# A two-layer block on one core: the triangular solve in blocks of 32 rows, one weight split on GpSimd, and the pair of FFN inputs interleaved in SBUF

## The reference

```python
def _rwkv7_step(S, inp):
    r, w, k, v, a, b = inp
    sa = jnp.einsum('bhvk,bhk->bhv', S, a)
    S = S * w[:, :, None, :] + sa[..., None] * b[:, :, None, :] + v[..., None] * k[:, :, None, :]
    y = jnp.einsum('bhvk,bhk->bhv', S, r)
    return S, y
...
    mean = jnp.mean(y, axis=-1, keepdims=True)
    var = jnp.mean(jnp.square(y - mean), axis=-1, keepdims=True)
    yn = ((y - mean) * lax.rsqrt(var + LNX_EPS)).reshape(B, T, D) * lnx_w + lnx_b
    bonus = (jnp.sum(rh * kh * r_k, axis=-1, keepdims=True) * vh).reshape(B, T, D)
    out = ((yn + bonus) * g).astype(x.dtype)
    return out @ w_o

def conv_ffn(x, w_in, conv_w, conv_b, w_out):
    T = x.shape[1]
    gate, up = jnp.split(x @ w_in, 2, axis=-1)
    gp = jnp.pad(gate, ((0, 0), (CONV_W - 1, 0), (0, 0)))
    gc = conv_b
    for j in range(CONV_W):
        gc = gc + gp[:, j:j + T, :] * conv_w[j]
    h = jax.nn.gelu(gc) * up
    return h @ w_out
```

## Time and profile before

| | |
|---|---|
| median of 3 runs | 1096.93 us (1094.85 to 1100.52) |
| the profiled execution, its own time | 1099.76 us |
| its span | 1097.9 us |
| granted clock, mean | 0.997 |
| PE busy | 1071.0 us (98%) |
| DVE busy | 801.8 us (73%) |
| ACT busy | 605.1 us (55%) |
| POOL busy | 209.3 us (19%) |

### The profile page before, as it was taken

The page is one execution under the profiler, slowest core; times in us unless marked ns, Lnnn a source line. Parts: engine busy times, 40 slices in busy tenths (PEclk is TensorE's granted clock), DMA queues, the critical chain, the costliest instruction groups (busy, mean ns, idle before and its releaser), DMA issues.

```text
span 1097.9 us, 19100 instructions
## 1 busy us (share of the span) xinstructions
PE 1071.0 (98%) x7335; PEld 924.8 (84%) x7335; DVE 801.8 (73%) x1134; ACT 605.1 (55%) x928; POOL 209.3 (19%) x230
## 2 busy tenths in 40 slices
PE   7999989999999999999999999999999999999997
PEld 6997788888888889789888888998777789888886
DVE  7997887778885758777788746688867776655543
ACT  6765354556664566856566544635665445545532
POOL 0134552112221011001222200470100001122200
PEclk9999999999999999999999999999999999999999
DMA  8553181646666566345667575456452654666552
GB/s 250 170 170 115 46 262 43 172 116 192 185 189 228 196 148 161 118 130 146 188 188 194 174 286 158 155 192 213 148 140 83 194 166 131 184 189 191 192 191 77
DMA packets 219748, 183.13 MB, mean 167 GB/s; under 512 B 43265, under 2 KB 197614, under 8 KB 219678
## 3 DMA queue, kind: packets, MB, share of 16 engines
q1 hardware_dynamic: 215710, 171.43, 52.1%
q0 software_dynamic: 3392, 8.66, 2.5%
q10 hardware_dynamic: 576, 2.07, 0.5%
HBM read 179.44 MB, written 2.69 MB: 166 GB/s over the span
## 4 chain that ended last, share of the span: by engine, by line
PE 82%; DVE 12%; issue 2%; ACT 1%; POOL 1%; DMA 1%; SPq 0%; DVEq 0%; POOLq 0%; ACTq 0%
PE bank L288 21%; PE bank L282 13%; PE bank L284 13%; PE bank L283 13%; PE bank L289 10%; PE bank L295 3%; DVE ring L413 3%; PE bank L1238 2%; DVE arena L1655 1%; DVE arena L1750 1%; DVE stat L1748 1%; PE bank L371 1%; PE bank L2123 1%; PE bank L1353 1%; DVE arena L1680 0%
## 5 line engine op out<-in xcount | busy, mean ns | idle before, releaser
L413 DVE TENSOR_TENSOR ring<-ring,arena 128x2048 fp32r<-128x2048 f32 (+1 forms) x138 | 312.3, 2266 | 113.0 <-ACT arena L407 111.4
L282 PE MATMUL bank<-arena 128*128 128x512 f32 (+3 forms) x980 | 343.8, 351 | 2.0 <-DVE ring L413 1.6
L288 PE MATMUL bank<-arena 128*128 128x512 f32 x960 | 339.8, 399 | 0.0
L407 ACT ACTIVATE arena<-ring 128x2048 fp32r<-128x2048 f32 (+1 forms) x145 | 272.0, 1879 | 93.0 <-DMA ring<-in_ffn_w_out 43.2
L289 PE MATMUL bank<-arena,ring 128*128 128x256 f32 x960 | 269.6, 281 | 0.0
L284 PE MATMUL bank<-arena 128*128 128x512 f32 (+3 forms) x720 | 264.9, 368 | 0.0
L288 PEld LDWEIGHTS bank<-arena 128*128 128x128 f32 x960 | 180.4, 188 | 44.7
L283 PE MATMUL bank<-ring,arena 128*128 128x512 f32 (+2 forms) x560 | 216.2, 386 | 0.0
L282 PEld LDWEIGHTS bank<-arena 128*128 128x128 f32 x980 | 185.5, 189 | 27.1 <-issue 3.7
L289 PEld LDWEIGHTS bank<-arena,ring 128*128 128x128 f32 x960 | 181.5, 189 | 0.0
L284 PEld LDWEIGHTS bank<-arena 128*128 128x128 f32 x720 | 135.6, 188 | 22.3
(11 more groups left out here) (335 smaller groups left out, 1282.7 us busy)
## 6 DMA issues: line engine op xcount, KB each, us to landing
ring<-in_ffn_w_in SPq DMA_DIRECT2D x80, 512.0 KB, 5.1
ring<-in_ffn_w_out SPq DMA_DIRECT2D x44, 512.0 KB, 4.4
ring<-in_w_gate_up SPq DMA_DIRECT2D x40, 512.0 KB, 5.1
ring<-in_w_in SPq DMA_DIRECT2D x18, 1024.0 KB, 5.0
ring<-in_a_w_rkv SPq DMA_DIRECT2D x12, 1024.0 KB, 5.5
ring<-in_w_down SPq DMA_DIRECT2D x22, 512.0 KB, 3.7
ring<-in_a_w_o SPq DMA_DIRECT2D x4, 1024.0 KB, 8.4
arena<-in_ffn_w_in SPq DMA_DIRECT2D x8, 512.0 KB, 4.7
```

The lines of the kernel that those rows point to most:

```text
L282: nc.tensor.matmul(dst, stationary[0], moving[0], start=start, stop=False)
L288: nc.tensor.matmul(dst[:, :], stationary[0], both_parts, start=start, stop=False)
L407: nc.scalar.activation(buf(hi_of(n), 0, w, arena12), ring[:, r, 0:w], ACT.Copy).then_inc(hi_ready, 1)
L413: on.tensor_tensor(ring12[:, r, 0:w], ring[:, r, 0:w], buf(hi_of(n), 0, w, arena12).bitcast(F32), ALU.subtract).then_inc(split_ready, 1)
```

## The change

- **Solve.** `sweep` and `summed` are replaced by `block_sweep(a, parts)`, which makes only the 32 rows of one block `b` for one group of heads, a 32 x 64 matmul for each head, and `block_added(a, g, b)`, with which DVE adds those 32 rows in place to the right side. The two groups are a stage apart: (0,1), then (0,2) with (1,1), (0,3) with (1,2), (1,3). `block_inverses(a, g)` is the product by `z`. `steps` leave out the first 32 columns.
- **Last slot of w_v.** DVE splits only at `j` 8 (slot 2). POOL subtracts the low part of the last slot as soon as slot 2 is split and the high part is there.
- **Bonus and centring.** `bonus_added` on DVE and `centred` on ACT are gone. ACT scales the values head by head (`bonus_scaled`), POOL subtracts the means (`values_centred`) and adds, gates and scales in three instructions for each tile instead of two (`rest_gated`).
- **Order.** On PE, `o_turn` of a part comes later; on DVE, the state, the variances and the low parts change places; on SP the first w_o slot is asked for ahead of the second copy of the inverses, and the FFN's early weights wait for `ymm` and `c_ready`.
- **FFN input.** High and low part lie side by side, interleaved by chunk (`(c x t)`), in buffers 11 and 12 or 10 and 11, so the moving operand of L288 is one run of 512.

```diff
-        def beside(i, j):
-            i, j = sorted((i, j))
-            return arena12[0][:, i:j + 1:j - i, :].rearrange("p s (c t) -> p s c t", t=T)
+        def beside(i):
+            return bufs(i, 2, arena12).rearrange("p (c x t) -> p c x t", x=2, t=T)
+
+        def parts_of(i):
+            pair = beside(i)
+            return pair[:, :, 0, :], pair[:, :, 1, :]
...
-        FFN_H, FFN_H_LO, FFN_F, FFN_F_LO, FFN_CONV, FFN_P = (12, 0, 0), (10, 5, 5), 1, 6, 4, 9
+        FFN_H, FFN_F, FFN_F_LO, FFN_CONV, FFN_P = (11, 10, 11), 1, 6, 4, 9
...
-                        mm = product_twice(bank[pair + g], both(w, slice(None), k, g), h2[0][:, k], h_parts[:, :, k],
+                        mm = product_twice(bank[pair + g], both(w, slice(None), k, g), h2[0][:, k], h_parts[:, k],
...
-                    mm = nc.tensor.matmul(bank[4 + b % 4][:, i * P:(i + 1) * P], z[a][:, h, :], n_off[a][:, h, :],
+                    mm = nc.tensor.matmul(bank[4 + b % 4][:, i * P + BS:(i + 1) * P], z[a][:, h, :], n_off[a][:, h, BS:P],
...
+            def block_sweep(a, parts):
+                for g, b in parts:
+                    if b > 1:
+                        pe.wait_ge(sum_ready, SUM_NO[a][g, b - 1])
...
+                for i in range(8):
+                    for g, b in parts:
+                        h, cells = 8 * g + i, rows_of_block(b)
+                        mm = nc.tensor.matmul(bank[g][cells, i * N:(i + 1) * N], n_off[a][:, h, cells],
+                                              rhs[a][:, h * N:(h + 1) * N], start=True, stop=True)
...
-                if j == 8 or j == 16:
-                    ahead(dve, FIRST["w_v"] + j // 8 + 1, split_dve)
+                if j == 8:
+                    ahead(dve, FIRST["w_v"] + 2, split_dve)
...
-            def summed(a, s):
-                for g in range(2):
-                    cells = slice(g * HALF, (g + 1) * HALF)
-                    dve.wait_ge(sweep_mm, sweeps_before(a, s) + g + 1)
-                    nc.vector.tensor_tensor(sums[a][:, cells], bank[g][:, :], rhs[a][:, cells], ALU.add).then_inc(sum_ready, 1)
+            def block_added(a, g, b):
+                rows, cells = rows_of_block(b), slice(g * HALF, (g + 1) * HALF)
+                dve.wait_ge(sweep_mm, SOLVED * a + SWEEP_NO[g, b])
+                nc.vector.tensor_tensor(rhs[a][rows, cells], bank[g][rows, :], rhs[a][rows, cells], ALU.add).then_inc(sum_ready, 1)
...
+            pool.wait_ge(split_ready, SPLIT_NO[FIRST["w_v"] + 2] + 1)
+            split_pool(pool, LAST["w_v"])
...
+            def rest_gated(a):
+                g = toks(W_G)[:, a, :]
+                chunks = lambda m: m.rearrange("p (c t) -> p c t", t=P)
+                pool.wait_ge(bonus_copied, NT + a + 1)
+                nc.gpsimd.tensor_tensor(rest[a], bonus[a], chunks(buf(W_LNX, D, 2 * D)), ALU.add).then_inc(c_ready, 1)
+                pool.wait_ge(c_ready, 3 * a + 1)
+                nc.gpsimd.tensor_tensor(rest[a], rest[a], chunks(g), ALU.mult).then_inc(c_ready, 1)
+                pool.wait_ge(c_ready, 3 * a + 2)
+                nc.gpsimd.tensor_tensor(g, g, buf(W_LNX, 0, D), ALU.mult).then_inc(c_ready, 1)
...
                 elif (a, s) == (0, 2):
-                    o_turn(1, 0)
                     pe.wait_ge(o_split, 2)
                 elif (a, s) == (0, 3):
-                    o_turn(1, 1)
+                    o_turn(1, 0)
                 elif (a, s) == (1, 0):
                     pe.wait_ge(o_split, 3)
+                elif (a, s) == (1, 1):
+                    o_turn(1, 1)
```

More of the change, by code:

```diff
@@ L450, in turn_dve @@
         def turn_dve(dve, turn, a, base, hi, lo=None, parts=(0, 1)):
+            hi, lo = (chan(x, arena12) if isinstance(x, int) else x for x in (hi, lo))
             for q in parts:
@@ L1366, in sweep @@
                         pe.wait_ge(u_rhs, g + 1)
-                    elif s == 1:
-                        pe.wait_ge(sum_ready, sums_before(1, 0) + g + 1)
-                    else:
[L1370 to L1374, removed]
-                        mm = by_columns(bank[SWEEP_BANK[a][s - 1] + g][:, i * N:(i + 1) * N], (z if last else n_off)[a][:, h, :],
-                                        (rhs if s == 1 else sums)[a][:, h * N:(h + 1) * N], True, True)
@@ L1379, in y_values, with block_inverses @@
+            def block_inverses(a, g):
+                pe.wait_ge(z_landed, (NT + a + 1) * 16 * NB)
+                pe.wait_ge(sum_ready, SUM_NO[a][g, NB - 1])
+                for i in range(8):
+                    h = 8 * g + i
+                    mm = by_columns(bank[(0, 4)[a] + g][:, i * N:(i + 1) * N], z[a][:, h, :], rhs[a][:, h * N:(h + 1) * N],
+                                    True, True)
+                mm.then_inc(sweep_mm, 1)
             def y_values(a, q):
@@ L1433, in rwkv_pe @@
                 nc.tensor.matmul(cells, bh[:, hv], u[0][:, hv], start=True, stop=False)
-                mm = nc.tensor.matmul(cells, kh[:, hv], v[:, 0, hv], start=False, stop=True)
+                mm = nc.tensor.matmul(cells, kh[:, hv], centred[0][:, hv], start=False, stop=True)
             mm.then_inc(state_mm, 1)
             y_solved(0, 0)
-            y_solved(0, 1)
+            y_values(0, 1)
             pe.wait_ge(state_ready, 2)
@@ L1444, in rwkv_pe @@
                     mm.then_inc(rem_mm, 1)
+            y_solved(0, 1)
+            block_sweep(1, ((0, 1),))
             pe.wait_ge(v_evac, 4 + NT)
@@ L1628, in o_evac @@
                                      bank[O_TURNED[q]][:, :].rearrange("p (c t) -> p c t", t=P), ACT.Copy).then_inc(o_in, 1)
-            centred(0)
-            solutions(0)
+            for b in range(5):
+                step_evac(b)
+            bonus_scaled(0, 0)
+            for b in range(5, STEP_BANKS):
+                step_evac(b)
+            act.wait_ge(sweep_mm, SWEEP_NO[1, 3])
             ahead(act, FIRST["w_o"], split_act)
-            centred(1)
+            solutions(0, 0)
+            solutions(0, 1)
+            bonus_scaled(0, 1)
+            bonus_scaled(1, 0)
             squares(0, 0)
+            bonus_scaled(1, 1)
             squares(0, 1)
-            act.wait_ge(state_mm, 1)
             ahead(act, FIRST["w_o"] + 2, split_act)
-            act.wait_ge(sweep_mm, sweeps_before(1, 1) + 1)
+            act.wait_ge(sweep_mm, SOLVED + SWEEP_NO[1, 2])
             ahead(act, LAST["w_o"], split_act)
-            solutions(1)
+            solutions(1, 0)
+            solutions(1, 1)
             o_evac(0, 0)
@@ L1814, in rwkv_dve @@
             centred_values(1)
[L1815 to L1835 removed]
+            value_means(0)
+            block_added(0, 0, 1)
+            value_means(1)
+            block_added(0, 0, 2)
+            block_added(0, 1, 1)
+            block_added(0, 0, 3)
+            block_added(0, 1, 2)
             centred_values(2)
+            block_added(0, 1, 3)
             centred_values(3)
@@ L1918, in rwkv_pool @@
                 nc.gpsimd.tensor_tensor(y_rstd[:, stat], y_var[:, stat], minus_half[:, 0:8], ALU.pow).then_inc(rstd_ready, 1)
+            values_centred(0)
+            values_centred(1)
+            pool.wait_ge(lnx_landed, 32)
+            rest_gated(0)
+            rstd(0)
+            rstd(1)
+            rest_gated(1)
+            rstd(2)
+            rstd(3)
         def rwkv_blocks_sp(sp):
@@ L3333, in weights_sp @@
             rwkv_inverse_sp(sp)
+            rows_of("w_o", A["a_w_o"][0], 2, range(0, 1))
             rwkv_inverse_late_sp(sp, 0)
-            rows_of("w_o", A["a_w_o"][0], 2, range(0, 2))
+            rows_of("w_o", A["a_w_o"][0], 2, range(1, 2))
             rwkv_inverse_late_sp(sp, 1)
             rows_of("w_o", A["a_w_o"][0], 2, range(2, 4))
-            sp.wait_ge(sweep_mm, sweeps_before(0, SWEEPS + 1) + 2)
+            sp.wait_ge(ymm, 2)
+            sp.wait_ge(c_ready, 4)
             early_in(0, 0, A["ffn_w_in"][0])
```

160 lines of the change are left out of this document (77 added, 83 removed).

## The result

The changed kernel takes 1108.09 us (median of 4 runs, 1105.37 to 1111.21) beside 1098.43 us for the one before. The ratio is 1.0108, with a 95% interval of 1.0081 to 1.0136: slower, where I had forecast 6 us less. The profiled execution has a span of 1104.9 us for 1097.9 before.

The account below looks back on a forecast made before the run. PE, busy 98% of the span, was taken as the bound. First layer -0.1 us and FFN input -6.3 sum to -6.4, so 1090.5 us from a median of 1096.93; range 1085.5 to 1099.5.

Parts of the forecast that it names:

- the FFN input: FFN pairs of L288 and L289: one run of 512 removes the operand's jump, -6.3 us, ends -6.3 and 0.
- the split: Inversion: last w_v split on POOL saves DVE 2.2 us but delays its loop 4.4; net +2.2 us.
- PE's saving in the solves: Two solves: 32-row blocks save PE 4.9 us, steps of 96 columns 1.9; -6.8 us, ends -2.6 and -6.8.
- step 4: Between solves and first w_o tile: exposed DVE block additions cost +1.8 us; "issue" pauses left out, -4.3.
- alternation of long and short matmuls: FFN pairs: alternation costs the 6.6 ns, so the layout does nothing; 1096.8 us, chance 0.33.
- the 42% of L935: Inversion: small DVE instructions lose 42% of POOL's overlap, giving the split's lower delay, 1.9 us.
- my third rival: First layer: POOL's SBUF products hold DVE beside w_o splits and gating, 6.5 us more; slower, chance 0.10.
- The "issue" pauses of 4.3 us: Before the w_o product: PE's unexplained idle of 1.68 and 2.62 us, left out of the layout as -4.3.
- step 6: First layer: idle "issue" partly returns and the clock may dip again; +2.6 us, ends 0 and 5.7.
- Given back behind: w_o product: PE, arriving earlier, waits for DVE at (0,3), (1,1) and (1,3); +4.4 us, ends +2.5 and +6.
- shift as one block: Behind the start of the last w_o tile (1,3): everything keeps its order and only shifts.

Follow-up runs that it names:

- e1: Kernel before with only the FFN input's new layout, one run of 512; ratio 0.9989 to before.
- e5: Kernel before, unchanged, profiled once more; 1092.41 us.
- e8: e2 with DVE's split of the second w_o slot ahead of the first tile's low part; ratio 1.0040 to before.
- e4: Changed kernel with GpSimd's masking product held until the inversion's loop is done; ratio 1.0053 to before.
- e2: Changed kernel with the last w_v split back on DVE; ratio 1.0043 to before.
- e3: Kernel before with only the last w_v split moved to GpSimd; ratio 1.0075 to before.
- e10: e2 with means and a variance behind added blocks, second w_o split earlier, GpSimd's second-tile products held; ratio 1.0011 to before.
- e11: e10 with PE's last transposes of the gated output at tile (1,0) instead of (1,1); ratio 1.0016 to before.
- e7: e2 with GpSimd's three second-tile products held until DVE has gated the first tile; ratio 1.0046 to before.
- e12: e11 with GpSimd's second-tile products right behind the first's, and DVE's first gating behind the last block addition; ratio 1.0020 to before.

## Why the prediction was wrong

The forecast was 6.4 us less. Two terms failed by their mechanism: the FFN input (-6.3), whose cause was not the jump in the operand, and the split (+2.2), which I let delay the inversion once, where it leads into a second stop and costs 6.9 us. Two more were mis-sized: PE's saving in the solves (-6.8, measured -3.8) and the waits of step 4 (+1.8, measured +6 and more). In the order of the prediction:

1. **FFN input, -6.3 us: the cause was wrong.** I had named the jump in the operand, against alternation of long and short matmuls, which was my rival. Neither is fixed. A stream of pairs runs in one of two rhythms, 110.9 or 113.0 us for 320 pairs, and keeps it through an FFN. With two runs of 256, 5 of 12 FFNs were fast (four profiled executions: 0, 1, 3 and 1 of 3); with one run of 512, 19 of 30 (ten executions). These shares can't be told apart, and the timed ratio of e1 leaves the layout between -3.1 and +0.7 us. Over the 42 FFNs no other length occurs, but for 0.1 us. Nor do the shares part on one chip: on that of e5 to e8 3 of 3 against 7 of 9, on that of e1 to e4 1 of 3 against 5 of 9. Whether the chip has a part in the rhythm is open. The step failed at its start: I took one execution's distance for a property of the code.
2. **The split, +2.2 us: right in size, incomplete.** e4 shows +2.1. The Trainium skill ("SBUF — State Buffer", section Who interferes with whom), which I had weighed there, calls the ports that DVE and GpSimd share an exclusive lock; DVE's 4.77 us beside a split of 4.61 agrees, and the 42% of L935 does not hold for this pair. What I left out is where the delay leads: the loop's end moved past 126.68 us, into GpSimd's next product, and was stopped again, for 4.47 us where 0.3 is usual. The earlier trace rows showed the memset up to 126.4, right at the loop's end. With the clock and pauses behind it the split cost 6.9 us at the first pair (changed kernel less e2) or 9.0 (e3 less before).
3. **PE's work, -6.8 us: -3.8.** A part with 16 matmuls of 32 x 64 takes 1.0 to 1.1 us, one with 8 takes 1.0, so a tile's four take about 4.2 us for 6.06. The lower price was right only where two groups run side by side. The steps gained nothing: 16 halves of 96 columns take 1.96 us and 8 take 1.06, so 112 ns for one more; with 128 columns it was 3.77 us for 32 and 1.98 for 16, again 112 ns. The Trainium skill ("TensorE: Matmul & The Clock Gate", section LDWEIGHTS (loading the stationary operand)) has the time to load a stationary operand grow with its columns, about 107 ns for 128 by its formula; the measured 112 ns at either width agrees with a bound by loading; no run varies the stationary operand alone.
4. **Waits between the solves and the w_o product, +1.8 us: +6 and more.** In e2 the gaps before its blocks are 0.8, 1.5 and 4.6 us. The last two come from DVE instructions that GpSimd's new products stop (L1803, L1811, L1813); the first stands behind the mean L1839, stopped for 2.66 us by a masking product and a memset that the kernel before has too. That is my third rival's mechanism: at chance 0.10 and priced 6.5 us it was there, for the gating, which the rival names, and for the variance, but not for the splits. The "issue" pauses of 4.3 us, which I took out here and put back by 2.6 in step 6, were absent in e2's solves; this was the part that went better than forecast. It isn't the change's doing alone: the kernel before had only 1.5 and 1.7 us of them in e5, and e10 has one of 1.7.
5. **Given back behind, +4.4 us: +3.4.** From the first w_o tile to the first pair it is 39.8 us before and 43.2 in e2. The two waits inside were 1.4 and 1.8 us, for 1.8 and 1.6 written, and 2.4 before the last tile. e11 shows that the last one hangs on the transposes at (1,1).
6. **Issue and clock, +2.6 us: about +2.1 in e2.** There are no pauses, but the clock is at half behind the gap of 4.6 us, which costs the 2.1 us that e7 has back. In the changed kernel the same stands in the second solve, and half clock also behind the long wait of the inversion.

The first layer came to +9.0 us at the first pair instead of -0.1: 6.9 from the split, 2.1 from the rest, which is again the sum of -3.8 and -4.3 gained and some 10 us lost in waits and at half clock. That GpSimd's products make the gap of 4.6 us is shown by e7; that removing it doesn't shorten the program is shown too. So the rest of +2.1 belongs to DVE's row of work up to the first tile's post-norm as a whole, and e10 to e12 take it back at the first pair by order alone.

The first pair isn't the end of the account. I had let all that follows shift as one block. From the last pair of the first FFN to the first of the second it is 170.6 or 170.7 us in the four profiled executions that solve by sweeps (before, e5, e1, e3), and 171.1 to 172.3 in the ten that solve by blocks of 32 rows. In e2 PE waits 1.05 us there, at 421.1 us, for a DVE instruction (L2386) that it does not wait for before. These 0.5 to 1.7 us are part of why e10 to e12, level or ahead at the first pair, are 0.1 to 0.2% behind in the timed runs. The profile adds up with it: 9.0 + 1.4 behind the first FFN + 0.7 behind the second - 4.2 that the FFNs of this execution were faster is 6.9 us, for the 7.0 measured.

Left open: what sets the rhythm of the pairs in an execution, and what delays the stretch behind the first FFN.

## What to carry to other kernels

Before work is moved to GpSimd "beside" DVE, list DVE's instructions in that stretch by their operands. Here those with two in SBUF stopped until GpSimd's instruction was over, and so did small TENSOR_SCALARs; additions with one in PSUM went on. A serial loop of small instructions pays the whole of it. Then move the delayed end forward in time and look at what GpSimd does there, for a delay can run into GpSimd's next instruction. A difference of a few ns in a long stream's distances should be seen in a second execution before a cause is given to it.

## What the runs showed of the hardware that I had not expected

- The pairs of a 512-column and a 256-column matmul took 346.6 ns in some FFNs and 353.1 in others, constant over 320 pairs, with the same code in two executions (e5: 110.9 us in all three FFNs; the profile before: 113.0 in all three). The three FFNs together make 6.3 us of spread, about as much as the scatter of the kernel's runs (1094.85 to 1100.52).
- A DVE TENSOR_SCALAR of 128 x 16 values, all in SBUF and with one tensor operand, took 2.73 us beside GpSimd (0.17 elsewhere). It ended with GpSimd's memset at 149.5 us, not with the product at 148.6. It is so in the other traces as well: in e2 it ended at 142.39, the memset at 142.36 and the product at 141.47; in the kernel before one of 128 x 32 values, begun at 140.67, took 1.33 us and ended at 142.00, the memset at 141.96 and the product at 141.07. That the memset, which reads nothing, stopped it too is how I read these rows; no run tests it alone.
- GpSimd is stretched in return: its product of 2.36 us took 4.32 and 4.34 beside DVE's splits in e7.
